# A hybrid diffusion step on one core: mLSTM running maxima spread by DRAM reads, and a step's exponents, exponentials and weighted keys made one step sooner

## What is computed

```
b = cumsum(log_f);  d = where(causal, b_t - b_s + i_s, NEG)
mt = maximum(b + m, max(d))
s = (q k^T) * exp(d - mt)
num = exp(b + m - mt) * (q C) + s v
h = num / maximum(|den|, exp(-mt))
C_new = decay * C + (wk * k)^T v
```

## Time and profile before

| | us |
|---|---|
| median of 3 runs | 1112.24 (1111.88 to 1113.05) |
| the profiled execution's own time | 1113.42 |
| its span in the profile | 1111.6 |
| PE busy | 1095.0 (99% of the span) |
| DVE busy | 805.8 (72%) |
| ACT busy | 535.2 (48%) |
| POOL (GpSimd) busy | 89.5 (8%) |

### The profile page before, as it was taken

How to read it: one execution, slowest core, us unless ns; L and a number is a source line. 1 busy time by engine, 2 the same in 40 slices (tenths; PEclk the granted TensorE clock), 3 DMA queues, 4 the chain that set the end, 5 groups by cost and what they waited for, 6 DMA issues and landing times.

```text
span 1111.6 us, 18544 instructions
## 1 busy us (share of the span) xinstructions
PE 1095.0 (99%) x7088; PEld 1029.7 (93%) x7088; DVE 805.8 (72%) x1430; ACT 535.2 (48%) x1027; POOL 89.5 (8%) x148
## 2 busy tenths in 40 slices
PE   6999999999999999999999999999999999999997
PEld 4799998889999999999999889999999999888886
DVE  5757987679769688886788547999987777633434
ACT  5534453545564345555553248555555555433431
POOL 2042333000000021010000012000000000000002
PEclk9999999999999999999999999999999999999999
DMA  9675653353611203544266344234322322424112
GB/s 363 242 234 146 184 179 114 115 152 100 73 58 42 73 20 102 184 146 124 78 217 210 103 154 165 76 118 149 115 77 85 125 95 77 133 77 170 57 38 95
DMA packets 42775, 140.74 MB, mean 127 GB/s; under 512 B 9376, under 2 KB 10944, under 8 KB 41152
## 3 DMA queue, kind: packets, MB, share of 16 engines
q1 hardware_dynamic: 38752, 131.64, 37.1%
q0 software_dynamic: 3936, 7.92, 2.3%
HBM read 126.89 MB, written 12.60 MB: 125 GB/s over the span
## 4 chain that ended last, share of the span: by engine, by line
PE 98%; ACT 1%; DMA 1%; DVE 0%; issue 0%; SPq 0%; POOL 0%; POOLq 0%; ACTq 0%
PE ps L2436 30%; PE ps L2437 30%; PE ps L2438 30%; PE ps L2751 1%; PE ps L2766 1%; PE ps L2725 1%; PE ps L2626 1%; PE ps L2628 1%; PE ps L2630 1%; DMA xt<-in_x_sample 1%; PE ps L2692 1%; PE ps L2495 0%; PE ps L2607 0%; PE ps L2726 0%; PE ps L2822 0%; PE ps L2513 0%
## 5 line engine op out<-in xcount | busy, mean ns | idle before, releaser
L2438 PE MATMUL ps<-h_hi,w_lo 128*128 128x320 f32 x880 | 271.9, 309 | 0.0
L2437 PE MATMUL ps<-h_lo,w_hi 128*128 128x320 f32 x688 | 212.6, 309 | 0.0
L2436 PE MATMUL ps<-h_hi,w_hi 128*128 128x320 f32 x624 | 195.5, 313 | 0.0
L2438 PEld LDWEIGHTS ps<-h_hi,w_lo 128*128 128x128 f32 x880 | 165.2, 188 | 0.0
L2436 PE MATMUL ps<-w_hi,h_hi 128*128 128x512 f32 x418 | 164.9, 394 | 0.0
L2438 PE MATMUL ps<-w_hi,h_lo 128*128 128x512 f32 x418 | 162.8, 390 | 0.0
L2437 PE MATMUL ps<-w_lo,h_hi 128*128 128x512 f32 x418 | 162.8, 389 | 0.0
L1719 DVE TENSOR_TENSOR w_lo<-raw,w_hi 128x1024 fp32r<-128x1024 f32 x85 | 102.9, 1221 | 47.2 <-ACT w_hi L1246 46.5
L2437 PEld LDWEIGHTS ps<-h_lo,w_hi 128*128 128x128 f32 x688 | 129.2, 188 | 0.1
L1246 ACT ACTIVATE w_hi<-raw 128x1024 fp32r<-128x1024 f32 x85 | 88.5, 1053 | 65.5 <-PE ps L2438 63.3
L2436 PE MATMUL ps<-h_hi,w_lo 128*128 128x320 f32 x384 | 119.1, 310 | 0.0
(11 more groups left out here) (314 smaller groups left out, 2129.3 us busy)
## 6 DMA issues: line engine op xcount, KB each, us to landing
raw<-in_w_blocks SPq DMA_DIRECT2D x182, 512.0 KB, 4.0
ada<-in_w_first SPq DMA_DIRECT2D x8, 1024.0 KB, 19.4
gdram<-stage SPq DMA_DIRECT2D x8, 640.0 KB, 6.7
gt<-gdram SPq DMA_DIRECT2D x8, 640.0 KB, 5.0
xline<-x SPq DMA_DIRECT2D x5, 512.0 KB, 5.0
x<-xline SPq DMA_DIRECT2D x5, 512.0 KB, 8.1
xt<-in_x_sample SPq DMA_DIRECT2D x4, 512.0 KB, 6.6
vg<-vline POOLq DMA_DIRECT2D x32, 64.0 KB, 3.5
```

The lines of the kernel that those rows point to most:

```text
L2436: nc.tensor.matmul(dst, wh, xh, start=first, stop=False, skip_group_check=resumed)
L2437: nc.tensor.matmul(dst, wh, xl, start=False, stop=False, skip_group_check=resumed)
L2438: return nc.tensor.matmul(dst, wl, xh, start=False, stop=last, skip_group_check=resumed)
```

## The change

- The matmul that spreads the maxima (L2601) goes, and with it `mpair`, `selp`, two of three columns of `parity`, the remainder rows of `mnat` and a memset on POOL. `mnat` becomes plain float32.
- At `mnat` POOL stores the running maxima to a DRAM tensor `mline` by two DMAs (one for each direction). At `mcols` SP waits for both and reads the rows of three pairs of steps, each by one DMA that repeats 512 values to 128 partitions (`mrow`, three buffers, 256 KB each). Seven more such reads follow, one at each even `ml` step up to 14; each waits until the exponents that used the buffer before are made.
- DVE makes the exponents from `mrow` in SBUF (`ml_exponents`): those of steps 0 and 1 in `ml` 0, and those of step n+2 in `ml_sum(n)`, right behind `num_sb`.
- ACT makes the weighted keys and the exponentials of step n+1 in `ml` n (`step_keys`, `decays`), ahead of the copy of the turned keys of step n+1; in `ml` 0 also those of step 0, ahead of the copy of the scores.
- On PE `ml_scores` is there at first visits only, and waits for the copied keys alone.

The diff, cut to its core:

```diff
-        mpair = at("mpair", [P, 2, (odd - even) // 4], even, F32R)[:, :, 0:T]
         MG = _e - 5120 - 20480
+        mrow = [at(f"mrow{i}", [P, MH, P], o) for i, o in enumerate((even, odd, MG + 22528))]
...
-        mnat = at("mnat", [P, T], R1 + 2560 * 7, F32R)
+        mnat = at("mnat", [RW, T], R1 + 2560 * 7)
...
+
+            def load_rows(j):
+
+                ch, dr, _, _, _ = ML_UNITS[2 * j]
+                if j >= len(mrow):
+                    sp.wait_ge(ml_dm, 2 * (j - len(mrow)) + 2)
+                src = bass.AP(mline.tensor, (dr * TT + ch) * MH * P, [[0, P], [1, MH * P]])
+                sp.dma_start(mrow[j % len(mrow)].rearrange("p h t -> p (h t)"), src).then_inc(mrow_in[j % len(mrow)], 16)
 
...
+                elif step[0] == "mcols":
+                    sp.wait_ge(m_line, 32)
+                    for j in range(len(mrow)):
+                        load_rows(j)
                 elif step[0] == "ml" and 1 <= step[1] <= 4:
+                    if step[1] in (2, 4):
+                        load_rows(step[1] // 2 + 2)
...
+                elif step[0] == "ml" and step[1] % 2 == 0 and 4 < step[1] < len(ML_UNITS) - 4:
+                    load_rows(step[1] // 2 + 2)
                 elif step[0] == "ada_store":
...
-                    nc.gpsimd.memset(mnat[:, :].bitcast(F32), 0.0).then_inc(fills, 1)
...
+                elif step[0] == "mnat":
+                    pool.wait_ge(stat_rd, 3)
+                    for dr in range(2):
+                        src = mnat[32 * dr:32 * dr + MH, :].rearrange("r (c t) -> r c t", t=P)
+                        pool.dma_start(mline[dr].rearrange("c r t -> r c t"), src).then_inc(m_line, 16)
...
-                    act.wait_ge(ml_a, FIRST_VISITS[o - 1] + 1)
+                    act.wait_ge(ml_a, o)
                 nc.scalar.activation(kt, ps[:, 3, 256:512].rearrange("p (i t) -> p i t", i=2), ACT.Copy).then_inc(kt_rd, 1)
...
+            def step_keys(n):
+
+                ch, dr, hp, _, _ = ML_UNITS[n]
+                if n > 1:
+                    act.wait_ge(ml_b, n - 1)
+                for i in range(2):
+                    r = dr * 4 + 2 * hp + i
+                    hd = 2 * hp + i
+                    ins = nc.scalar.activation(kw_sb[:, n % 2, i, :], mk[:, ch, hd * P:(hd + 1) * P], ACT.Copy,
+                                               scale=mcols[:, ch, 2, r:r + 1])
+                ins.then_inc(ml_kw, 1)
+
+            def decays(n):
+
+                act.wait_ge(ml_dm, n + 1)
+                nc.scalar.activation(e_sb[:, n % 2], e_sb[:, n % 2], ACT.Exp, scale=-1.0).then_inc(ml_e, 1)
 
             def first_sum(n):
...
                 elif step[0] == "mcols":
                     turned_keys(0)
-                    act.wait_ge(stat_rd, 3)
-                    for i in range(2):
-                        ins = nc.scalar.activation(mpair[:, i, :], mnat[:, :].bitcast(F32), ACT.Copy,
-                                                   scale=parity[:, i:i + 1])
-                    ins.then_inc(pair_rd, 1)
...
                         ch, dr, hp, _, _ = ML_UNITS[n]
-                        act.wait_ge(ml_a, n + 1)
                         if n == 0:
                             act.wait_ge(ms_rd, 3)
+                            step_keys(0)
+                            decays(0)
                         if n in FIRST_VISITS:
+                            act.wait_ge(ml_a, FIRST_VISITS.index(n) + 1)
                             nc.scalar.activation(scores[:, scores_held(ch, hp)],
                                                  ps[:, 3, 0:256].rearrange("p (i t) -> p i t", i=2),
                                                  ACT.Copy).then_inc(ml_sc, 1)
-                        act.wait_ge(ml_dm, n + 1)
-                        nc.scalar.activation(e_sb[:, n % 2], e_sb[:, n % 2], ACT.Exp, scale=-1.0).then_inc(ml_e, 1)
...
-                    if n < len(ML_UNITS):
-                        ch, dr, hp, _, _ = ML_UNITS[n]
-                        for i in range(2):
-                            r = dr * 4 + 2 * hp + i
-                            hd = 2 * hp + i
-                            ins = nc.scalar.activation(kw_sb[:, n % 2, i, :], mk[:, ch, hd * P:(hd + 1) * P], ACT.Copy,
-                                                       scale=mcols[:, ch, 2, r:r + 1])
-                        ins.then_inc(ml_kw, 1)
+                    if n + 1 < len(ML_UNITS):
+                        step_keys(n + 1)
+                        decays(n + 1)
                     if n + 1 in FIRST_VISITS:
                         turned_keys(n + 1)
...
+            def ml_exponents(n):
+
+                ch, dr, hp, _, _ = ML_UNITS[n]
+                slot = n // 2 % len(mrow)
+                dve.wait_ge(mrow_in[slot], 16 * (n // 2 // len(mrow) + 2))
+                for i in range(2):
+                    r = dr * 4 + 2 * hp + i
+                    ins = nc.vector.scalar_tensor_tensor(e_sb[:, n % 2, i, :], mrow[slot][:, 2 * hp + i, :],
+                                                         mcols[:, ch, 0, r:r + 1], mask_m[:, dr, :],
+                                                         ALU.subtract, ALU.max)
+                ins.then_inc(ml_dm, 1)
...
             def ml_sum(n):
...
+                if n + 2 < len(ML_UNITS):
+                    ml_exponents(n + 2)
...
-                    for i in range(3):
-                        columns = ident[:, i:P:2] if i < 2 else ident
-                        ins = nc.vector.tensor_reduce(parity[:, i:i + 1], columns, X, ALU.add)
-                    for q in (0, 64):
...
+                    nc.vector.tensor_reduce(ones_col[:, :], ident, X, ALU.add).then_inc(stat_rd, 1)
...
-                    dve.wait_ge(fills, 5)
-                    link(turned(mnat, st[3]))
-                    nc.vector.tensor_tensor(mnat[64:96, :], st[3][0:32, :], mnat[0:32, :].bitcast(F32), ALU.subtract)
-                    for lo, hi in spans:
-                        ins = nc.vector.tensor_tensor(mnat[96:64 + RW, lo:hi], st[3][32:RW, lo:hi][:, ::-1],
-                                                      mnat[32:RW, lo:hi].bitcast(F32), ALU.subtract)
-                    ins.then_inc(stat_rd, 1)
+                    turned(mnat, st[3]).then_inc(stat_rd, 1)
...
                     dve.wait_ge(state_in, 16)
                 elif step[0] == "ml":
                     n = step[1]
-                    if n < len(ML_UNITS):
-                        ch, dr, hp, _, _ = ML_UNITS[n]
-                        dve.wait_ge(ml_a, n + 1)
-                        for i in range(2):
-                            r = dr * 4 + 2 * hp + i
-                            ins = nc.vector.scalar_tensor_tensor(e_sb[:, n % 2, i, :], A[2][:, i * P:(i + 1) * P],
-                                                                 mcols[:, ch, 0, r:r + 1], mask_m[:, dr, :],
-                                                                 ALU.subtract, ALU.max)
-                        ins.then_inc(ml_dm, 1)
+                    if n == 0:
+                        ml_exponents(0)
...
                                                 ALU.mult).then_inc(ml_st, 1)
                     if n:
                         ml_sum(n - 1)
+                    else:
+                        ml_exponents(1)
...
             def ml_scores(n):
 
                 ch, dr, hp, _, _ = ML_UNITS[n]
-                if n:
-                    pe.wait_ge(ml_dm, n)
-                else:
+                if n == 0:
                     pe.wait_ge(ms_rd, 3)
-                    pe.wait_ge(stat_rd, 1)
-                    pe.wait_ge(pair_rd, 1)
-                ins = nc.tensor.matmul(A[2][:, 0:256].rearrange("p (i t) -> p i t", i=2),
-                                       selp[:, dr, hp:hp + 1].to_broadcast([P, P]), mpair[:, :, tok(ch)],
-                                       start=True, stop=True)
-                if n in FIRST_VISITS:
-                    pe.wait_ge(kt_rd, FIRST_VISITS.index(n) + 1)
-                    for i in range(2):
-                        ins = nc.tensor.matmul(ps[:, 3, i * P:(i + 1) * P], kt[:, i, :], mq[:, 2 * hp + i, tok(ch)],
-                                               start=True, stop=True)
+                pe.wait_ge(kt_rd, FIRST_VISITS.index(n) + 1)
+                for i in range(2):
+                    ins = nc.tensor.matmul(ps[:, 3, i * P:(i + 1) * P], kt[:, i, :], mq[:, 2 * hp + i, tok(ch)],
+                                           start=True, stop=True)
                 ins.then_inc(ml_a, 1)
 
...
-                    if step[1] < len(ML_UNITS):
+                    if step[1] in FIRST_VISITS:
                         ml_scores(step[1])
```

20 lines of the change are left out of this document (9 added, 11 removed).

## The result

| | us |
|---|---|
| kernel before, median of 13 runs | 1113.05 (1111.88 to 1114.16) |
| changed kernel, median of 13 runs | 1115.02 (1113.90 to 1115.97) |
| ratio | 1.0019, 95% interval 1.0012 to 1.0026 |
| forecast: difference | +1.8 |
| measured: difference (0.19% of 1113.05) | +2.1 (1.3 to 2.9) |

The change makes the kernel about 2 us slower, close to what was forecast. The waits that were forecast are there, beside a late start of DVE that was not foreseen, and several terms missed in ways that cancel.

What follows compares the result with a forecast made beforehand. PE, busy 99% of the span, was taken to bound the kernel. -2.4 + 1.2 (A) + 1.8 (B) + 1.2 (C) = +1.8 us, from a median of 1112.24 to 1114.0 us; range 1110.8 to 1116.6.

Steps and rivals of the forecast that it cites:

- What comes off PE: The 20 spreading matmuls leave PE, each worth 0.12 us to the next matmul's start: -2.4 us.
- Sooner by 1.7 us on DVE and SP: Ahead of step 0, DVE's w_lo and SP's raw load come up to 1.7 us sooner, near 267.1 and 268.3.
- A: PE's wait at step 1's scores, behind the first mrow read (landing 272.4) and a 3.15 us chain: +1.2 us.
- B: PE's wait for step 4's turned keys, copied behind exponentials that wait for DVE's exponents: +1.8 us.
- the three steps: Within B: the loop lengthens by 0.55 to 0.6 us in each of three steps, 1.75 together.
- the 0.25 us "to spare": Within B: slack between the copy of step 4's turned keys and PE's coming at 288.78, subtracted from the delay.
- C: The stretch from 342 to 360 where DVE is full and PE goes at DVE's pace: +1.2 us.
- The part for the saving that isn't kept: Within C: the 0.12 us of each of steps 14 to 17 is not kept, 0.5 us.
- The part for the new order: Within C: exponents now come behind num_sb, straight ahead of bo_lo, which PE's next tile reads; 0.7 us.
- Costed at nothing: POOL's two stores, the seven later reads and exponents reading SBUF instead of PSUM were taken to cost nothing.
- the second: Rival: the first read doesn't queue behind the weight block, lands near 271.2; total +0.6, 1112.8 us; chance 0.10.
- The third: Rival: B's loop has spare time and DVE fits the exponents into idle time; -2.4, 1109.8 us; chance 0.13.

Runs made afterwards that it cites:

- e5: The kernel before with the matmul that spreads the maxima issued twice in each of the 20 steps; 1115.06 us, ratio 1.0020.
- e3: The changed kernel with the first mrow read issued ahead of the fourth raw block in SP's queue; 1113.03 us, ratio 1.0001.
- e6: The changed kernel with ACT's exponentials and weighted keys back in the step of their use, DVE's exponents still one step sooner; 1115.14 us, ratio 1.0022.
- e2: The changed kernel with exponents, exponentials and weighted keys back in their old step and order, maxima still from DRAM; 1112.59 us, ratio 0.9995.
- e7: e6 plus the first read ahead of the fourth raw block and the turned keys' copy ahead of the weighted keys; 1112.75 us, ratio 0.9999.
- e10: e9 without the seven one-column DVE copies; 1111.09 us, ratio 0.9987.
- e9: e7 with DVE's exponents back in their old place and seven one-column DVE copies added at mstat; 1110.27 us, ratio 0.9980.
- e8: The changed kernel with seven one-column DVE copies added at mstat; 1114.38 us, ratio 1.0014.
- e11: The changed kernel with the seven one-column DVE copies at ml 20, behind the mLSTM's last exponents; one execution, 1114.30 us.
- e12: The changed kernel with the spare place of seven columns but without any copies; one execution, 1115.72 us.
- e1: The changed kernel with the turned keys' copy on ACT moved ahead of the next step's weighted keys and exponentials; 1113.57 us, ratio 1.0003.
- e4: e1 with the next step's exponents made at the end of DVE's step instead of between num_sb and bo_lo; 1117.79 us, ratio 1.0042.

## Why the prediction was right, point by point

- **What comes off PE**, -2.4: held. e5 measured +2.2 for 20 more.
- **Sooner by 1.7 us on DVE and SP**: it was 2.2 for both (`w_lo` at 266.6 and the block at 267.9 in the time of the kernel before). The read's landing, 272.4 by estimate, was 272.5, by luck in part: the read landed 1.1 us behind the block and not 0.5. e3 shows that the landing sets A.
- **A**, +1.2: it was 1.9. The mechanism and the landing were right, the chain was 0.4 us too short by a late start of `st_sb` that no row of the trace before could show, and PE's restart adds 0.2.
- **B**, +1.8: it was 1.7, at the place and in the order that were described, and e3 shows that it is its own wait. Its sum was right by two misses: the three steps put the copy of the turned keys 1.46 us later against PE, not 1.75, and the 0.25 us "to spare" were the time from ACT to PE. 1.46 + 0.24 gives the 1.7. What the forecast didn't have is that ACT's new order isn't needed for it: e6, with ACT's old order, loses 1.82.
- **C**, +1.2: it was 0.64. The part for the saving that isn't kept was put at 0.5 and is 0.40 (e2). The part for the new order was put at 0.7 and is 0.24 (the changed kernel against e2). With the exponents alone one step sooner, as in e6 and e7, C is 1.86 and 1.84: that ACT's exponentials go with them wins most of it back, since `st_sb` then needn't wait for them, as I read it.
- **Costed at nothing**: POOL, the later reads and the operand in SBUF cost nothing, as said. But the count of DVE's instructions, which I did not cost at all, was worth 0.7 us of the measured 2.1: 0.35 in A and 0.35 near 679. That A came out higher, C lower and that this was missing cancelled nearly, so that the sum is better than its terms is luck.
- **The rivals**: a read ahead of the weight block's landing (the second) did not happen by itself, and e3 shows what it would have been worth. The third, waits covered, needed the exponents back in their place, the first read early and the keys' copy sooner on ACT: it is e10, and e9 with the copies.

## What to carry to other kernels

To make something one step sooner on engines that work in order is to put a wait for it ahead of everything that stands behind it there: look at what is queued behind the waiting instruction (here the turned keys' copy and the weight block's upper half), not at the result that comes sooner. When an operation is taken off the bounding engine, measure that by itself first: here the reordering that came with it cost 2.7 us (the changed kernel against e2). Even alone it kept only 0.6 of 2.4 us, since the first read landed late and the turned keys' copy came just in time for PE; with both moved sooner and the count of DVE instructions as before (e9) it kept 2.2. A gap on another engine is time to spare only if it is longer than the time that the hand-over takes in a row where somebody waits. Put the first small read ahead of a large one in the same queue, and, when a few tenths matter, compare the idle time of the same instruction far behind the change as well.

## What the runs showed of the hardware

- A DVE instruction at certain places of its stream can start 0.35 us late: 0.46 us instead of 0.10 to 0.12 behind its releaser. Near 676 the idle time is 1.26 us in all nine kernels with 1423 DVE instructions, and 0.91 in those with 1430 (the kernel before, e5, e8, e9, e11). It moves with the number of instructions ahead (e8, e11), neither with time nor with addresses (e12; e11 and e12 ran once). The place alone isn't enough: `st_sb` of step 0 is late where the copy of the scores ends its wait (1.18 to 1.20 us of idle time in the changed kernel, e1, e3, e4, e11 and e12, against 0.83 in e8, which has the seven copies), and not in e2 and e6, where the exponentials end it (0.48, as before). What happens in these 0.35 us no row names; that it is the loading of DVE's instructions was not tried and stays open.
- A 256 KB read that repeats 2 KB of DRAM to 128 partitions landed in 3.0 us when the last 512 KB block ahead of it had been issued 2.9 us before (e3), and in 4.3 us when that was 0.4 us before. The rule of the Trainium skill, "DMA: Bandwidth & Descriptors", section "Anatomy of one DMA — SWDGE (gpsimd) path", gives an estimate of 2.6 us; both are above it.
- PE loses 0.1 to 0.2 us more than its idle time at a wait (A: 1.90 against 1.72; B in e3: 1.64 against 1.51). The first matmuls behind it last longer: the scores' four matmuls 0.71 us behind wait A, 0.61 in `ml` 0.
